# Second attention of a two-block transformer kernel: the halves of the output projection's weight chunks one head apart, the values ahead of the next transposes, the last queries copied at once

## The chip, the cores and the metric

One core of a Trainium2 chip runs the whole program. The metric is the device time in microseconds (us) of one execution. The time before the change is the median of three runs.

## What is computed

The reference runs 256 tokens of width 1024 through two blocks. The first has sliding-window and block attention and a feed-forward network. The second adds 16 meta tokens and has two layers of feed-forward networks around a pooling mixer in the first layer and a latent attention in the second. Only this latent attention is touched by the change:

```python
def mla_attention(h, w_dq, q_latent_norm, w_uq, w_o, k_nope, k_rope, v, cos, sin):
    cq = rmsnorm_2(h @ w_dq, q_latent_norm)
    q = (cq @ w_uq).reshape(B, L, N_HEADS, QK_NOPE + QK_ROPE)
    ...
        s = (jnp.einsum('bqhd,bkhd->bhqk', qn, k_nope)
             + jnp.einsum('bqhr,bkr->bhqk', qr, k_rope)).astype(jnp.float32) * sm_scale
        s = jnp.where(mask[None, None], s, jnp.finfo(jnp.float32).min)
        p = jax.nn.softmax(s, axis=-1).astype(v.dtype)
        return jnp.einsum('bhqk,bkhd->bqhd', p, v)
    ...
    return o @ w_o
```

There are 8 heads, 64 features without and 32 with rotary positions, 64 features of values, and the output projection w_o is 512 by 1024. After the attention comes the last feed-forward network ("ffn2_1"), and the final norm.

## The kernel before

**Weights.** All weights come from memory in chunks of 8 tiles of 128 by 128 (512 KB), in one order, into a ring of 8 raw buffers. SyncE issues the transfers in order and waits, before it reuses a buffer, until the low half of the chunk that lay in it has been made. A dense product is made of three passes: ScalarE copies a chunk to its high half (`split_hi`, line 1139), VectorE subtracts that from the raw chunk to get the low half (`split_lo`, line 1512), and TensorE multiplies high by high, high by the low half of the activations, and low by high (lines 615, 616 and 617). The halves lie in rings of 5 buffers. `split_hi(i)` waits for the transfer and for the last matmul that reads chunk i-5; `split_lo(i)` waits for `hi_done`; the matmuls wait for `lo_done`. In the attention, the places where the splits stand are written out by hand in each engine's order. The chunks are numbered here from the first of the output projection: chunks 0 to 3 are w_o, chunk -2 holds the rotary queries of heads 4 to 7 and part of the last keys, chunk -1 the rest of these keys and the last queries without rotary part, and chunks 4 and 5 are the first of ffn2_1.

**The order of the attention.** There is no planner; each engine runs its own list in order, and the loop `for i in range(MH + 2)` (MH = 8 heads) is written once for each engine, with semaphores between them.

- TensorE, step i: `scores2(i)` into a bank of PSUM (two banks, in turn), the transposes of head i-2 (`transposes2`, one bank, so it waits for `pT2_done` of the head before), and in even steps from 4 the values of a pair of heads (`values2`), which wait for the copied transposes of both heads and for the output of the pair before to be read out. Between them stand dense products that fill time: `uq_rope(1)` in step 0, `keys(1)` in step 1, `uq_nope(1)` (the queries of heads 4 to 7) in step 2, `out_proj(0)` in step 6, `out_proj(1)` in step 8. After the loop come half of `out_proj(2)`, `values2(3)`, the other half, and `out_proj(3)`.
- VectorE, step i: the maxima of head i's scores (line 2008) and the shift (line 2011), the reciprocals and the weights' scaling of head i-1 (lines 2017 and 2020), then whatever belongs to this step: `q_rope(1)` in step 0 (line 1973), `k_nope(1)` in step 2 (line 1968), `q_nope(1)` in step 3 (line 1964), the low half of a pair's output in odd steps from 5 (line 2029), and the low half of a chunk: 0, 1, 2, 3 in steps 0 to 3, 4 and 5 in steps 8 and 9. Chunk -1 is made just ahead of the loop.
- ScalarE, step i: the copy of the transposes of head i-2 (`pT2`, line 1467), the exponentials of head i (line 1474), then `k_nope(1)` in step 1, `q_nope(1)` in step 2 (line 1439), the high half of a pair's output in even steps from 4 (line 1484), and the high half of the same chunk as VectorE in the same step.
- `scores2(i)` waits for the exponentials of head i-2, and `scores2(4)` also for both halves of the `q_nope(1)` copies (ScalarE takes the even heads and VectorE the odd ones, after it). `transposes2(h)` waits for the scaled weights of head h. `exponentials` of head i wait for the shift, and from head 4 on for the transposes that free the buffer of the weights. From head 4 on the `pT2` copy also waits for the values of two pairs before.
- GpSimd adds the rotary parts of heads 4 to 7 (line 2183) after `q_rope(1)`.

Of the kernel before, what the change touches and what calls it, by code (L numbers as in the profile page):

```python
# [30 lines left out]
MH, ROPE = 8, 32  # L31
# [358 lines left out]
def build_program(nc, xT, metaT, vecs, consts, bands, bias_oh, bias_rows, wstream, scratch, outT):  # L390
# [6 lines left out]
    with ctx:  # L397
# [147 lines left out]
        weights2 = lambda h, n: p2[:, h // 2 % 2, p2_at(h, n):p2_at(h, n) + KW[n]]  # L545
        turned = lambda ap: ap.rearrange("p h (b t) -> p h b t", b=2)[:, :, ::-1, :]
        in_blocks = lambda ap: ap.rearrange("p h (b t) -> p h b t", b=2)
        WO_SPLITS = {i: i for i in range(4)}
        WO_SPLITS.update({MH: 4, MH + 1: 5})
        wo_out = lambda t: G[plan.pair["wo_a" if t < 4 else "wo_b"]][:, t // 2 % 2, t % 2 * SEQ:(t % 2 + 1) * SEQ]  # L550
        wo_left = lambda t: plan.left_dve["wo_a"] - 3 + t
        POOL_SPLITS = {0: 3, 1: 4, 4: 5, 6: 6}
# [38 lines left out]
        def tensor_program(e):  # L591
# [416 lines left out]
            def scores2(i):  # L1008
                bank = A[(i + 1) % 2]
                if i == 0:  # L1010
                    e.wait_ge(left_act, plan.left_act["uk0"])
                    e.wait_ge(left_dve, plan.left_dve["uk0"])
                    e.wait_ge(khead_rope, 1)
                    e.wait_ge(rows_set, 2)
                    e.wait_ge(q_var, 1)
                elif i == 1:
                    e.wait_ge(mix_var, 1)
                else:
                    e.wait_ge(exp2_done, i - 1)
                if i == 4:  # L1020
                    e.wait_ge(left_act, plan.left_act["uqn1"])
                    e.wait_ge(left_dve, plan.left_dve["uqn1"])
                if i < 2:
                    e.wait_ge(qrot_done, i + 1)
                else:
                    e.wait_ge(qrot_pool, i - 1)
                for n in (1, 0):
                    m = e.matmul(bank[:, OFF[n]:OFF[n] + KW[n]], qhead[:, i, n * P:(n + 1) * P], khead[:, i, KEYS(i, n)], start=True, stop=True)  # L1028
                m.then_inc(scored2, 1)
# [21 lines left out]
            def values2(p):  # L1051

                o = o2_of(p)
                if p == 0:
                    e.wait_ge(vm_act, 1)
                    e.wait_ge(vm_dve, 1)
                else:
                    e.wait_ge(o2_lo, p)
                e.wait_ge(pT2_done, 2 * p + 2)
                def meta(n):  # L1060
                    rows = slice(n * HD, n * HD + 2 * META)
                    return e.matmul(o[:, n * P:(n + 1) * P], v_meta[rows, p * P:(p + 1) * P], pT2[rows, (2 * p + 1) % 4, 3 * P:4 * P], start=n == 0, stop=n == 1, skip_group_check=True)
                meta(0).then_inc(meta_first, 1)
                for h in (2 * p, 2 * p + 1):
                    oh_, cols = o[h % 2 * HD:(h % 2 + 1) * HD, :], slice(h * HD, (h + 1) * HD)
                    e.matmul(oh_[:, 0:SEQ], v2[:, 0, cols], pT2[:, h % 4, 0:SEQ], start=False, stop=False, skip_group_check=True)
                    e.matmul(oh_[:, P:SEQ], v2[:, 1, cols], pT2[:, h % 4, SEQ:384], start=False, stop=False, skip_group_check=True)
                e.wait_ge(meta_first, p + 1)
                m = meta(1)
                m.then_inc(valued2, 1)  # L1070
# [20 lines left out]
            for i in range(MH + 2):  # L1091
                if i < MH:
                    scores2(i)
                if i >= 2:
                    transposes2(i - 2)
                if i >= 4 and i % 2 == 0:
                    values2((i - 4) // 2)
                if i == 0:
                    uq_rope(1)
                if i == 1:  # L1100
                    keys(1)
                if i == 2:
                    uq_nope(1)
                if i == 6:
                    out_proj(0)
                if i == MH:
                    out_proj(1)
# [20 lines left out]
        def scalar_program(e):  # L1128
# [316 lines left out]
                e.activation(in_blocks(khead[0:HD, 4 * i:4 * i + 4:2, 0:SEQ]), turned(src[:, :, META:T]), ACT.Copy).then_inc(left_act, 1)  # L1445
            split_hi(plan.last["uv"])
            q_nope(0)
            split_hi(plan.last["uqr1"])
            k_nope(0)
            e.wait_ge(q_var, 1)  # L1450
            e.activation(qsc[:, 2:4], qsc[:, 0:2], ACT.Sqrt, scale=float(QK)).then_inc(root_done, 1)
            preload(ACT.Exp)
            split_hi(plan.last["uqn1"])
            e.wait_ge(mm_done, ended["uv"])
            e.activation(v2[:, 0, :], G[plan.pair["uv"]][:, 0, :], ACT.Copy).then_inc(left_act, 1)
            e.wait_ge(mm_done, ended["uv_meta"])
            e.activation(values_of_pairs(v_meta, 0), values_of_pairs(A[3], 0), ACT.Identity, scale=con[:, cat["meta_of"]:cat["meta_of"] + 1]).then_inc(vm_act, 1)

            first_wo = steps["wo"][0].i
            for i in range(MH + 2):  # L1460
                if i >= 2:
                    h = i - 2
                    w = 512 if h % 2 else 384
                    e.wait_ge(transposed2, h + 1)
                    if h >= 4:
                        e.wait_ge(valued2, (h - 4) // 2 + 1)
                    e.activation(pT2[:, h % 4, 0:w], A[2][:, 0:w], ACT.Copy).then_inc(pT2_done, 1)
                if i < MH:
                    st = stat[:, i % 4, :]
                    e.wait_ge(shift2_done, i + 1)  # L1470
                    if i >= 4:
                        e.wait_ge(transposed2, 2 * ((i - 4) // 2) + 2)
                    for n in (1, 0):
                        a = e.activation(weights2(i, n), A[(i + 1) % 2][:, OFF[n]:OFF[n] + KW[n]], ACT.Exp,
                                         bias=st[:, n:n + 1], scale=qsc[:, n:n + 1], accum_out=st[:, 2 + n:3 + n])
                    a.then_inc(exp2_done, 1)
                if i == 1:
                    k_nope(1)
                if i == 2:
                    q_nope(1)  # L1480
                if i >= 4 and i % 2 == 0:
                    p = (i - 4) // 2
                    e.wait_ge(valued2, p + 1)
                    e.activation(o2h[:, p, :], o2_of(p), ACT.Copy).then_inc(o2_hi, 1)
                if i in WO_SPLITS:
                    split_hi(first_wo + WO_SPLITS[i])
            e.wait_ge(valued2, MH // 2)
            e.activation(o2h[:, 3, :], o2_of(3), ACT.Copy).then_inc(o2_hi, 1)
            preload(ACT.Sqrt)
# [13 lines left out]
        def vector_program(e):  # L1503
# [458 lines left out]
            def q_nope(i):  # L1962
                e.wait_ge(left_act, plan.left_act[f"uqn{i}"])
                e.tensor_copy(qhead[0:HD, 4 * i + 1:4 * i + 4:2, :], G[plan.pair[f"uqn{i}"]][HD:P, :, 0:SEQ]).then_inc(left_dve, 1)
# [24 lines left out]
            e.wait_ge(q_var, 1)  # L1989
            e.wait_ge(root_done, ROOT["latent_q"])  # L1990
            e.reciprocal(qsc[:, 0:2], qsc[:, 2:4]).then_inc(rstd_done, 1)
            e.wait_ge(mm_done, ended["uv"])
            e.tensor_copy(v2[:, 1, :], G[plan.pair["uv"]][:, 1, :]).then_inc(left_dve, 1)
            e.wait_ge(mm_done, ended["uv_meta"])
            e.wait_ge(vm_act, 1)
            e.tensor_scalar(values_of_pairs(v_meta, 1), values_of_pairs(A[3], 1), con[:, cat["meta_of"] + 1:cat["meta_of"] + 2], None, ALU.mult).then_inc(vm_dve, 1)
            split_lo(plan.last["uqn1"])

            first_wo = steps["wo"][0].i
            e.wait_ge(rstd_done, RSTD["latent_q"])  # L2000
            for i in range(MH + 2):
                if i < MH:
                    bank, st = A[(i + 1) % 2], stat[:, i % 4, :]
                    e.wait_ge(scored2, i + 1)
                    if i >= 4:
                        e.wait_ge(weighted2, i - 3)
                    for n in (1, 0):
                        a = e.tensor_reduce(st[:, 6 + n:7 + n], bank[:, OFF[n]:OFF[n] + KW[n]], AX_X, ALU.max, negate=True)
                    a.then_inc(max2_done, 1)
                    e.wait_ge(max2_done, i + 1)  # L2010
                    e.tensor_tensor(st[:, 0:2], st[:, 6:8], qsc[:, 0:2], ALU.mult).then_inc(shift2_done, 1)
                if i == 0:
                    q_rope(1)
                if 1 <= i <= MH:
                    st = stat[:, (i - 1) % 4, :]
                    e.wait_ge(exp2_done, i)
                    e.reciprocal(st[:, 4:6], st[:, 2:4]).then_inc(recip2_done, 1)
                    e.wait_ge(recip2_done, i)
                    for n in (1, 0):
                        a = e.tensor_scalar(weights2(i - 1, n), weights2(i - 1, n), st[:, 4 + n:5 + n], None, ALU.mult)  # L2020
                    a.then_inc(weighted2, 1)
                if i == 2:
                    k_nope(1)
                if i == 3:
                    q_nope(1)
                if i >= 5 and i % 2:
                    p = (i - 5) // 2
                    e.wait_ge(o2_hi, p + 1)
                    e.tensor_tensor(o2l[:, p, :], o2_of(p), f(o2h[:, p, :]), ALU.subtract).then_inc(o2_lo, 1)
                if i in WO_SPLITS:  # L2030
                    split_lo(first_wo + WO_SPLITS[i])
            e.wait_ge(o2_hi, 4)
            e.tensor_tensor(o2l[:, 3, :], o2_of(3), f(o2h[:, 3, :]), ALU.subtract).then_inc(o2_lo, 1)

# [218 lines left out]
```

## Time and profile before

| | us |
|---|---|
| median of 3 runs | 1285.72 (1284.29 to 1287.08) |
| the profiled execution, time | 1284.93 |
| the profiled execution, span | 1283.5 |
| TensorE busy | 1239.3 (97%) |
| VectorE busy | 879.7 (69%) |
| ScalarE busy | 633.7 (49%) |
| mean granted TensorE clock over the span | 0.989 of full |

The span is the time from the first to the last recorded instruction; the time lies 1.4 us above it. "Busy" counts an engine's own instructions, not its waits. The names "PE", "DVE", "ACT", "POOL" and "SP" stand for TensorE, VectorE, ScalarE, GpSimd and SyncE; "PEld" is TensorE's weight load, which overlaps its matmuls. The times in the rows are microseconds from the start of the span. A line of the timeline gives the start, the length, the engine, the line of the program, and in brackets the idle time before it and who ended that. The attention loop runs from about 1031 to 1085 us.

### The profile page before, as it was taken

Reading aid. Unit: us, or ns where it says so; the run is one execution under the profiler, and the core shown is the slowest. Engines: PE = TensorE matmul, PEld = TensorE weight load, DVE = VectorE, ACT = ScalarE, POOL = GpSimd, SP = SyncE. Lnnn points to the kernel's source line nnn. Section 1 sums busy time; section 2 is a strip of 40 time slices with the busy share of each in tenths; the row PEclk is TensorE's granted clock in tenths of the full one; section 3 lists DMA queues with packets and bytes.
Section 4 is the critical chain, followed back from the end, with each engine's and each line's share of the span. In section 5 each row is a group of like instructions: output and inputs, shape, how many; then the busy total and the mean of one; then the engine's idle time right before and its main releaser. Section 6 shows DMA issues by size and latency. Waiting matters only on the chain.

```text
span 1283.5 us, 23765 instructions
## 1 busy us (share of the span) xinstructions
PE 1239.3 (97%) x9924; PEld 1208.7 (94%) x9924; DVE 879.7 (69%) x1239; ACT 633.7 (49%) x986; POOL 178.6 (14%) x177
## 2 busy tenths in 40 slices
PE   4999999999999999999999999999999979999997
PEld 3988899999999999999999999999999968999997
DVE  7789979877566766655766665666667664766653
ACT  5545545766444444443544454445454455554531
POOL 2024424000231000012200002210001311000021
PEclk9999999999999999999999999999999978999999
DMA  8986565657555555654355555555564531656550
GB/s 326 322 310 215 198 223 204 241 214 280 181 183 175 165 169 177 198 173 127 118 195 167 182 178 181 181 164 183 196 201 158 185 98 34 197 184 196 183 163 33
DMA packets 67570, 239.16 MB, mean 186 GB/s; under 512 B 7366, under 2 KB 9592, under 8 KB 67464
## 3 DMA queue, kind: packets, MB, share of 16 engines
q1 hardware_dynamic: 66872, 235.46, 55.1%
q0 software_dynamic: 592, 2.19, 0.5%
q8 instruction: 78, 1.28, 0.4%
q14 instruction: 28, 0.23, 0.1%
HBM read 236.55 MB, written 1.07 MB: 185 GB/s over the span
## 4 chain that ended last, share of the span: by engine, by line
PE 86%; DVE 7%; ACT 2%; issue 1%; POOL 1%; DVEq 0%; ACTq 0%
PE G L615 26%; PE G L616 25%; PE G L617 25%; DVE sb_wlo L1512 2%; PE A L760 1%; PE A L735 1%; PE A L615 1%; ACT sb_whi L1139 1%; PE A L617 1%; PE A L616 1%; PE A L1028 0%; DVE sb_xl L2037 0%; DVE sb_hidf L1601 0%; PE G L1083 0%; PE A L746 0%
## 5 line engine op out<-in xcount | busy, mean ns | idle before, releaser
L1512 DVE TENSOR_TENSOR sb_wlo<-sb_raw,sb_whi 128x1024 fp32r<-128x1024 f32 (+1 forms) x398 | 486.4, 1256 | 90.3 <-ACT sb_whi L1139 90.0
L615 PE MATMUL G<-sb_xh,sb_whi 128*128 128x256 f32 (+2 forms) x1752 | 497.0, 284 | 5.1 <-DVE sb_wlo L1512 2.2
L616 PE MATMUL G<-sb_xl,sb_whi 128*128 128x256 f32 (+2 forms) x1752 | 496.7, 284 | 0.0
L1139 ACT ACTIVATE sb_whi<-sb_raw 128x1024 fp32r<-128x1024 f32 (+1 forms) x398 | 405.0, 1043 | 183.7 <-PE G L617 166.3
L617 PE MATMUL G<-sb_xh,sb_wlo 128*128 128x256 f32 (+2 forms) x1752 | 495.3, 283 | 0.0
L615 PEld LDWEIGHTS G<-sb_xh,sb_whi 128*128 128x128 f32 x1752 | 329.7, 188 | 8.3 <-issue 2.6
L617 PEld LDWEIGHTS G<-sb_xh,sb_wlo 128*128 128x128 f32 x1752 | 329.4, 188 | 0.0
L616 PEld LDWEIGHTS G<-sb_xl,sb_whi 128*128 128x128 f32 x1752 | 329.1, 188 | 0.0
L615 PE MATMUL G<-sb_hh,sb_whi 128*128 128x256 f32 (+1 forms) x1056 | 299.0, 283 | 0.6 <-DVE sb_hh L1732 0.6
L617 PE MATMUL G<-sb_hh,sb_wlo 128*128 128x256 f32 (+1 forms) x1056 | 298.0, 282 | 0.0
L616 PE MATMUL G<-sb_hl,sb_whi 128*128 128x256 f32 (+1 forms) x992 | 280.3, 283 | 0.0
L615 PEld LDWEIGHTS G<-sb_hh,sb_whi 128*128 128x128 f32 x1056 | 198.4, 188 | 1.0 <-issue 0.5
L617 PEld LDWEIGHTS G<-sb_hh,sb_wlo 128*128 128x128 f32 x1056 | 198.4, 188 | 0.0
L616 PEld LDWEIGHTS G<-sb_hl,sb_whi 128*128 128x128 f32 x992 | 186.5, 188 | 0.0
L1365 ACT ACTIVATE sb_gu<-sb_gu 128x272 f32<-128x272 f32 (+1 forms) x88 | 37.4, 425 | 191.5 <-DVE sb_gu L1840 191.3
L1840 DVE TENSOR_TENSOR sb_gu<-G,sb_rstd 128x544 f32<-128x544 f32 (+1 forms) x84 | 59.4, 707 | 59.8 <-PE G L617 59.8
L2079 POOL TENSOR_TENSOR sb_sumsq<-sb_X 128x256 f32<-128x256 f32 (+1 forms) x6 | 3.7, 622 | 651.6 <-DVE sb_X L1570 651.6
L1846 DVE TENSOR_TENSOR sb_hidf<-sb_gu 128x272 f32<-128x272 f32 (+1 forms) x88 | 38.3, 435 | 50.2 <-ACT sb_gu L1365 50.2
L1849 DVE TENSOR_TENSOR sb_hl<-sb_hidf,sb_hh 128x272 fp32r<-128x272 f32 (+1 forms) x88 | 38.2, 434 | 43.3 <-ACT sb_hh L1367 43.3
L1367 ACT ACTIVATE sb_hh<-sb_hidf 128x272 fp32r<-128x272 f32 (+1 forms) x88 | 37.4, 425 | 50.7 <-DVE sb_hidf L1846 50.7
L2084 POOL TENSOR_TENSOR sb_sq<-sb_X 128x256 f32<-128x256 f32 (+1 forms) x41 | 31.4, 766 | 203.7 <-DVE sb_X L1570 203.7
L2089 POOL TENSOR_TENSOR sb_sumsq<-sb_sumsq,sb_sq 128x256 f32<-128x256 f32 (+1 forms) x41 | 44.8, 1094 | 3.2
(328 smaller groups left out, 1289.1 us busy)
## 6 DMA issues: line engine op xcount, KB each, us to landing
sb_raw<-in_wstream SPq DMA_DIRECT2D x438, 512.0 KB, 4.4
sb_raw<-in_wstream SPq DMA_DIRECT2D x8, 320.0 KB, 6.9
sb_bias<-bias_scratch POOLq DMA_DIRECT2D x1, 2048.0 KB, 16.3
sb_X<-in_xT SPq DMA_DIRECT2D x2, 512.0 KB, 6.4
out_T<-sb_X SPq DMA_DIRECT2D x4, 256.0 KB, 2.7
sb_con<-in_consts SPq DMA_DIRECT2D x1, 601.0 KB, 8.7
sb_band<-in_bands SPq DMA_DIRECT2D x1, 314.0 KB, 5.0
sb_vec<-in_vecs SPq DMA_DIRECT2D x1, 82.5 KB, 2.0
```

Of the source, the lines that this page charges most:

```text
L615: e.matmul(out, w_h, xs, start=k0 + s.kt == 0, stop=False)
L616: e.matmul(out, w_h, xr, start=False, stop=False)
L617: m = e.matmul(out, w_l, xs, start=False, stop=k0 + s.kt == ktotal - 1)
L1139: e.activation(whi[:, i % NSPLIT, 0:w], raw[:, c % NRAW, 0:w], ACT.Copy).then_inc(hi_done, 1)
L1365: e.activation(gu[:, b, 0, 0:n], gu[:, b, 0, 0:n], ACT.Silu).then_inc(silu_done, 1)
L1367: e.activation(hh[:, j * n:(j + 1) * n], hidf[:, b, 0:n], ACT.Copy).then_inc(hid_hi, 1)
L1512: e.tensor_tensor(wlo[:, i % NSPLIT, 0:w], raw[:, c % NRAW, 0:w], f(whi[:, i % NSPLIT, 0:w]), ALU.subtract).then_inc(lo_done, 1)
L1840: e.tensor_tensor(gu[:, b, :, 0:n], G[plan.pair[name]][:, :, 0:n], rb, ALU.mult).then_inc(left_dve, 1)
L1846: e.tensor_tensor(hidf[:, b, 0:n], gu[:, b, 0, 0:n], gu[:, b, 1, 0:n], ALU.mult).then_inc(hid_mul, 1)
L1849: e.tensor_tensor(hl[:, sl], hidf[:, b, 0:n], f(hh[:, sl]), ALU.subtract).then_inc(hid_lo, 1)
L2084: e.tensor_tensor(s, src, src, ALU.mult).then_inc(sumsq_done, 1)
L2089: e.tensor_tensor(sumsq[:, cols], sumsq[:, cols], s, ALU.add).then_inc(sumsq_done, 1)
```

## The change

Four things are done, and the arithmetic stays the same.

1. The places of the splits. The high half of chunk -1 is made ahead of the first key copy, its low half ahead of the copy of the value rows; the high half of chunk 0 is made ahead of the loop, and its low half between the two value copies. In the loop a chunk's high half and its low half stand in different steps: high halves of chunks 1 to 5 in steps 0, 3, 5, 7, 8 of ScalarE, low halves in steps 1, 4, 6, 8, 9 of VectorE.
2. TensorE: `values2` stands ahead of `transposes2` in even steps from 4.
3. ScalarE: in these steps the exponentials and then the `pT2` copy, instead of the copy first.
4. VectorE: `q_nope(1)` at the start of step 3 instead of at its end.

```diff
-        WO_SPLITS = {i: i for i in range(4)}
-        WO_SPLITS.update({MH: 4, MH + 1: 5})
+        WO_HIGH, WO_LOW = {0: 1, 3: 2, 5: 3, MH - 1: 4, MH: 5}, {1: 1, 4: 2, 6: 3, MH: 4, MH + 1: 5}
...
                 if i < MH:
                     scores2(i)
+                if i >= 4 and i % 2 == 0:
+                    values2((i - 4) // 2)
                 if i >= 2:
                     transposes2(i - 2)
-                if i >= 4 and i % 2 == 0:
-                    values2((i - 4) // 2)
...
             q_nope(0)
-            split_hi(plan.last["uqr1"])
+            split_hi(plan.last["uqn1"])
             k_nope(0)
...
             preload(ACT.Exp)
-            split_hi(plan.last["uqn1"])
+            first_wo = steps["wo"][0].i
+            split_hi(first_wo)
...
+            def turned_weights(h):
+                w = 512 if h % 2 else 384
+                e.wait_ge(transposed2, h + 1)
+                if h >= 4:
+                    e.wait_ge(valued2, (h - 4) // 2 + 1)
+                e.activation(pT2[:, h % 4, 0:w], A[2][:, 0:w], ACT.Copy).then_inc(pT2_done, 1)
+
+            def exponentials(i):
+                st = stat[:, i % 4, :]
+                e.wait_ge(shift2_done, i + 1)
+                if i >= 4:
+                    e.wait_ge(transposed2, 2 * ((i - 4) // 2) + 2)
+                for n in (1, 0):
+                    a = e.activation(weights2(i, n), A[(i + 1) % 2][:, OFF[n]:OFF[n] + KW[n]], ACT.Exp,
+                                     bias=st[:, n:n + 1], scale=qsc[:, n:n + 1], accum_out=st[:, 2 + n:3 + n])
+                a.then_inc(exp2_done, 1)
             for i in range(MH + 2):
-                if i >= 2:
-                    h = i - 2
...
+                values_first = i >= 4 and i % 2 == 0
+                if i >= 2 and not values_first:
+                    turned_weights(i - 2)
                 if i < MH:
...
+                    exponentials(i)
+                if values_first:
+                    turned_weights(i - 2)
...
-                if i in WO_SPLITS:
-                    split_hi(first_wo + WO_SPLITS[i])
+                if i in WO_HIGH:
+                    split_hi(first_wo + WO_HIGH[i])
...
             e.reciprocal(qsc[:, 0:2], qsc[:, 2:4]).then_inc(rstd_done, 1)
+            split_lo(plan.last["uqn1"])
             e.wait_ge(mm_done, ended["uv"])
             e.tensor_copy(v2[:, 1, :], G[plan.pair["uv"]][:, 1, :]).then_inc(left_dve, 1)
+            first_wo = steps["wo"][0].i
+            split_lo(first_wo)
             e.wait_ge(mm_done, ended["uv_meta"])
...
-            split_lo(plan.last["uqn1"])
...
             for i in range(MH + 2):
+                if i == 3:
+                    q_nope(1)
...
-                if i == 3:
-                    q_nope(1)
...
-                if i in WO_SPLITS:
-                    split_lo(first_wo + WO_SPLITS[i])
+                if i in WO_LOW:
+                    split_lo(first_wo + WO_LOW[i])
```

## Rows read from the trace of the kernel before

**Rows 1.** The page: busy time, and the granted clock in 40 slices (tenths).

```profile
PE 1239.3 (97%) x9924; PEld 1208.7 (94%) x9924; DVE 879.7 (69%) x1239; ACT 633.7 (49%) x986; POOL 178.6 (14%) x177
...
PEclk9999999999999999999999999999999978999999
```

**Rows 2.** Busy time by stretch of the attention, all engines; PEclk is the granted clock.

```profile
1031.60:1037.40 5.80, 5.80 (x43) 5.38 (x41) 3.48 (x7) 2.54 (x6) 1.71 (x3) 1.00 0.35 101
1037.40:1041.00 3.60, 1.09 (x10) 1.05 (x10) 2.42 (x7) 2.12 (x7) 1.99 (x2) 1.00 0.46 130
1041.00:1044.40 3.40, 3.40 (x16) 3.28 (x16) 2.75 (x8) 1.71 (x5) 0.00 (x0) 0.50 0.24 55
1044.40:1047.80 3.40, 1.26 (x9) 0.72 (x8) 2.19 (x4) 2.20 (x5) 0.00 (x0) 1.00 0.29 116
1047.80:1063.50 15.70, 13.59 (x49) 9.15 (x49) 7.70 (x27) 7.08 (x21) 0.00 (x0) 0.50 0.24 68
1063.50:1068.30 4.80, 4.80 (x23) 4.80 (x23) 0.00 (x0) 0.38 (x1) 0.00 (x0) 0.50 0.00 0
1068.30:1071.70 3.40, 2.46 (x18) 1.76 (x16) 1.79 (x7) 1.44 (x5) 0.00 (x0) 1.00 0.00 0
1071.70:1084.70 13.00, 13.00 (x102) 11.23 (x102) 5.71 (x12) 6.86 (x15) 0.40 (x1) 1.00 0.27 82
```

**Rows 3.** Timeline of TensorE, 83 to 88 and 1036 to 1072 us: around its waits.

```profile
85.96 0.39 PE L615 MATMUL G<-sb_xh,sb_whi 128*128 128x256 f32 x1 [1.51 <-DVE sb_wlo L1512]
...
1036.58 0.87 PE L1028 MATMUL A<-sb_khead,sb_qhead 98*128 98x272 f32 x4
1039.95 0.55 PE L1040 MATMUL A<-sb_con,sb_p 128*128 128x128 f32 x3 [2.50 <-DVE sb_p L2020]
...
1049.91 1.73 PE L1028 MATMUL A<-sb_khead,sb_qhead 98*128 98x272 f32 x4 [4.25 <-DVE sb_qhead L1964]
...
1068.58 0.87 PE L1028 MATMUL A<-sb_khead,sb_qhead 98*128 98x272 f32 x4
1069.28 0.49 PE L1040 MATMUL A<-sb_con,sb_p 128*128 128x128 f32 x3
...
1071.16 0.52 PE L1040 MATMUL A<-sb_con,sb_p 128*128 128x128 f32 x3 [0.94 <-DVE sb_p L2020]
```

**Rows 4.** Timeline of TensorE at full clock, 1071 to 1078 us: starts of the pieces.

```profile
1071.61 0.48 PE L1062 MATMUL A<-sb_pT,sb_v_meta 32*128 32x128 f32 x2
...
1073.24 0.38 PE L1083 MATMUL G<-sb_o2h,sb_whi 128*128 128x256 f32 x1
...
1076.15 0.49 PE L1040 MATMUL A<-sb_con,sb_p 128*128 128x128 f32 x3
...
1077.02 0.39 PE L1083 MATMUL G<-sb_o2h,sb_whi 128*128 128x256 f32 x1
```

**Rows 5.** Timeline of VectorE ahead of the loop and in it.

```profile
1030.37 0.69 DVE L1993 COPY sb_v<-G 128x512 f32<-128x512 f32 x1 [1.48 <-PE G L635]
1032.35 0.48 DVE L1996 TENSOR_SCALAR sb_v_meta<-A,sb_con 128x256 f32<-128x256 f32 x1 [1.29 <-ACT sb_v_meta L1457]
...
1036.86 1.23 DVE L1512 TENSOR_TENSOR sb_wlo<-sb_raw,sb_whi 128x1024 fp32r<-128x1024 f32 x1 [1.54 <-ACT sb_whi L1139]
...
1038.96 0.94 DVE L2020 TENSOR_SCALAR sb_p<-sb_p,sb_stat 128x272 f32<-128x272 f32 x2
...
1047.41 0.66 DVE L2008 TENSOR_REDUCE sb_stat<-A 128x1 f32<-128x272 f32 x2
...
1048.96 0.69 DVE L1964 COPY sb_qhead<-G 64x512 f32<-64x512 f32 x1
```

**Rows 6.** Timeline of ScalarE in the loop.

```profile
1044.59 0.58 ACT L1439 ACTIVATE sb_qhead<-G 64x512 f32<-64x512 f32 x1
...
1048.29 0.58 ACT L1474 ACTIVATE sb_p<-A,sb_stat,sb_qsc 128x272 f32<-128x272 f32 x1 [1.70 <-DVE sb_stat L2011]
...
1049.31 1.05 ACT L1139 ACTIVATE sb_whi<-sb_raw 128x1024 fp32r<-128x1024 f32 x1
```

More of the change, by code:

```diff
@@ L1457, in scalar_program @@
             e.activation(values_of_pairs(v_meta, 0), values_of_pairs(A[3], 0), ACT.Identity, scale=con[:, cat["meta_of"]:cat["meta_of"] + 1]).then_inc(vm_act, 1)
-            first_wo = steps["wo"][0].i
-            for i in range(MH + 2):
-                if i >= 2:
-                    h = i - 2
[L1463 to L1467, printed above, removed]
-                if i < MH:
[L1469 to L1476, printed above, removed]
+            def turned_weights(h):
[13 more added lines that the diff above has]
+                a.then_inc(exp2_done, 1)
+            for i in range(MH + 2):
+                values_first = i >= 4 and i % 2 == 0
+                if i >= 2 and not values_first:
+                    turned_weights(i - 2)
+                if i < MH:
+                    exponentials(i)
+                if values_first:
+                    turned_weights(i - 2)
                 if i == 1:
@@ L1996, in vector_program @@
             e.tensor_scalar(values_of_pairs(v_meta, 1), values_of_pairs(A[3], 1), con[:, cat["meta_of"] + 1:cat["meta_of"] + 2], None, ALU.mult).then_inc(vm_dve, 1)
-            split_lo(plan.last["uqn1"])
-            first_wo = steps["wo"][0].i
             e.wait_ge(rstd_done, RSTD["latent_q"])
             for i in range(MH + 2):
+                if i == 3:
+                    q_nope(1)
                 if i < MH:
```

## The prediction, made before the changed kernel was run

> **What bounds the kernel now.** I read the page first: TensorE is busy 97% of the span, no other engine over 69%, and the granted clock is full but for two slices near the end [rows 1]. So time can only be won where TensorE stands still or runs at its low clock, and nearly all of that lies in the attention that the change touches. Second, busy time by stretch [rows 2]: of the 53.1 us from 1031.6 to 1084.7 TensorE is busy 45.4 (the eight rows add up to that), so it stands still for 7.7. Its clock is 0.50, the 1.2 GHz level, from 1041.0 to 1044.4 and from 1047.8 to 1068.3, which is 23.9 us, and 1.00 (2.4 GHz) in the other stretches. Third, TensorE's timeline [rows 3], for what ends the idle time: 2.50 us ahead of the first transposes, at 1039.95, until VectorE has scaled the weights of head 0; 4.25 us ahead of the scores of head 4, at 1049.91, until VectorE has copied the queries; 0.94 ahead of the last even transposes. The sum is 7.69. The first two stand right before the two falls of the clock; after the 0.94, and after the 1.51 us at 86 us, it stayed at full. Fourth, why VectorE is late [rows 5]: it waits 1.54 us for the high half of chunk 0 (1036.86), then makes the low half (1.23), and only then takes the maxima of head 1 and scales head 0 (1038.96, with 0.94, done at 1039.90). The high half, 1.05 us [rows 6], stands behind ScalarE's exponentials in the same step, so each of the steps 0 to 3 holds exponentials, high half and low half one after the other. The last query copy comes at 1048.96 after all of that [rows 5].
>
> **Prices of the pieces.** TensorE at full clock, from start to start: scores 0.70 ahead of transposes [rows 3], about 0.6 ahead of dense work (an estimate: dense matmuls start sooner behind them); even transposes 0.45, odd ones 0.87, values 1.63, 24 matmuls of the output projection 2.91 [rows 3, 4], so 0.12 each: about 2.2 for a product of 18 matmuls (`uq_rope`, `uq_nope`) and, with 272 columns, 1.6 for the 12 of `keys`. VectorE: from the maxima of a head (1047.41) to the query copy (1048.96) is 1.55 for maxima, shift, reciprocals and scaling, 0.88 of it until the exponentials start at 1048.29; copies of 512 columns 0.69, output low half about 0.45 (nearest row: 0.48) [rows 5, 6]. ScalarE: exponentials 1.02 from start to start, high half 1.05, query copy 0.58; copied transposes of like size 0.5 to 0.6, output high half about 0.4 (estimate, half of the columns) [rows 6].
>
> **Part by part, along TensorE's list.**
>
> *Ahead of the loop.* Low halves of chunks -1 and 0, 2.4 us, now stand around VectorE's value copies. These wait 1.48 and 1.29 us, together 2.77 [rows 5], and both high halves are there by then (that of chunk -1 fills ScalarE's wait for the first keys, that of chunk 0 takes its place). So they cost nothing, and VectorE is free for head 0 at 1032.8 (1032.35 and 0.48), 1.2 earlier. Without that cover they would cost what they cost now. Slots: chunk 0 needs chunk -5 to be read, chunk -1 chunk -6; both are finished long before.
>
> *The first gap (2.50).* VectorE's rotary product follows `uq_rope(1)`, done about 1034.5, to 1035.3; maxima of head 1 to 1036.1; head 0, whose exponentials ended near 1034.8, is scaled by 1036.8, or 1037.2 at the 0.94 of row 1038.96. TensorE ends the scores of head 2 at 1037.45 (1036.58 and 0.87). The gap is gone; `uq_nope(1)` runs from about 1037.6 to 1039.8, scores 3 and transposes 1 to 1041.5.
>
> *The second gap (4.25).* VectorE: low half of chunk 1 to 1038.0, maxima of head 2 to 1038.8, scaling of head 1, key copy to 1040.2. ScalarE: exponentials of head 2 until 1039.9, query copy 1040.0 to 1040.6. VectorE's query copy stands first in step 3: 1040.6 to 1041.3. Scores 4 start about 1041.6: 0.2 us of waiting instead of 4.25. The maxima of head 3 wait behind that copy for at most 0.7; who waits for them are the exponentials of head 3 and scores 5, which TensorE reaches only at 1044.2.
>
> *Values first, exponentials before the copied transposes.* Values 0 need the copies of heads 0 and 1 only (1042.0), so they fill the time in which head 2 is scaled. What is late next is the copy of transposes 2, ahead of transposes 3: ScalarE has the copy of head 1, exponentials 3 (1042.2 to 1043.2), the high half of chunk 2 (to 1044.2), exponentials 4 (to 1045.2) and then this copy, to 1045.7. TensorE is through with scores 5 at 1044.8 and waits 1.05. Behind transposes 3 and scores 6, values 1 wait 0.3 for the output of pair 0 to be read out.
>
> *Steps 6 to 9.* Transposes 4, `out_proj(0)` (2.9), scores 7 and transposes 5 run to 1054.0. Values 2 now stand ahead of transposes 6 and need pair 1's low half, which VectorE makes in step 7, after the maxima of head 7 and the scaling of head 6: 1053.4 plus 1.5 plus 0.45 is 1055.4. TensorE waits 1.5. Then values 2, transposes 6, `out_proj(1)`, transposes 7, half of `out_proj(2)`, values 3, the other half and `out_proj(3)` without a wait: 1.63 + 0.4 + 2.85 + 0.87 + 1.42 + 1.63 + 1.42 + 2.85 = 13.1 from 1055.5, which is 1068.7. The high halves of chunks 2 to 5 wait for slots freed by the values' rows, `keys(1)`, `uq_nope(1)` and `out_proj(0)`, all past by then; the low halves are ready before `out_proj(2)`, `out_proj(3)` and the feed-forward network ask for them.
>
> *SyncE's queue.* A transfer waits for the low half eight chunks before. Low halves -1 to 3 all come earlier by the clock than before, those of 4 and 5 some 10 us ahead of the next network, as now, so no transfer comes late. GpSimd's four rotary additions only need the rotary product, which stays where it was.
>
> **The sum, twice.** By the walk TensorE ends at 1068.7 instead of 1084.7: 16.0 saved. By the stretches: 23.6 us of busy time lie at full clock and 21.8 at half [rows 2]. 23 matmuls in 4.80 us against 24 in 2.91 make the low clock dearer by a factor of 1.72 [rows 2, 4], so 21.8 becomes 12.7, and 9.1 are won. The old idle time is 7.7; the new is 0.2 + 0.1 + 1.05 + 0.3 + 1.5 = 3.15, about 1 of which the ends of the running matmuls cover, so 2.2. Saved: 9.1 + 7.7 - 2.2 = 14.6. I take 15.3, the middle. Nothing behind the loop differs: the feed-forward network hangs on the last output tiles. The profiled execution took 1284.9, which gives 1269.6; the median shown lies 0.8 above it: **1270.4**.
>
> **Rivals.**
>
> *A, my forecast: both gaps go and the clock stays full.* For it: the stretch from 1068.30 to 1071.70 holds scores, two groups of transposes and a wait of 0.94, 2.46 us busy of 3.40, and kept 1.00; so did 86 us with 1.51. My worst stretch, 1044.4 to 1047.8, is busy about 2.1 to 2.3, against 1.09 and 1.26 before the falls. Own range 1268.5 to 1272.5: no new waits at all would give 2.2 less; a copy or two later in steps 5 to 7 would give 1 or 2 more.
>
> *B, the clock falls once inside the loop*, at the wait of 1.05 or at that of 1.5. Against it, the same rows; for it, nothing between 1.26 and 2.46 us busy has been seen here. Before, the level came back after dense products, after 3.4 us (`uq_nope`) and within the 4.8 of `out_proj(0)`. So the fall would last through values, transposes and one output product: 4.9 us of work become 8.4, and the scores behind add 1: plus 3.5 to 5, 1274 to 1275.5. The Trainium skill, page "TensorE: Matmul & The Clock Gate", section "A second HAM failure mode: psum-queue depth-cycling", says that many short idles between groups of matmuls can be enough for the clock to swing; that speaks for B, and only a trace of the new order can show it.
>
> *C, the first gap stays in part.* If scaling head 0 comes 1 us or more later than I have it (its margin is 0.3 to 0.6), the clock falls at 1041 as now, and no dense product follows before `out_proj(0)`: low from 1041 to about 1056, 15 us at a loss of 1 - 1/1.72 = 0.42 each is 6.3, and 0.7 of waiting: 1277.5.
>
> *D, slower than before.* The clock falls and does not come back before the loop ends, since less dense work lies together. To eat 15.3 us it would have to be low for 36 us, against 23.9 now: from 1041 through `out_proj(0)`, `(1)` and `(2)` and beyond. Both times that a dense product ran at the low level the clock came back [rows 2], and four such products follow. 1287.
>
> *E, no difference.* Only if the waits I remove come back whole elsewhere: 2.50 and 4.25 are each one engine's queue, and I find no second work of that size in front of them.
>
> **Chances.** A 0.75, B 0.13, C 0.07, D 0.03, E 0.02. A measurement of this kernel can tell 0.2%, 2.6 us, from no change. Faster: A, B and C, 0.95; same 0.02; slower 0.03. The range takes in A with the ends of its bounds and B: 1268.0 to 1275.8; C, D and E are left out.
>
> **What would show it.** TensorE's timeline: no wait over 0.5 us ahead of the first transposes or the scores of head 4; waits of about 1 us ahead of transposes 3 and of 1.5 ahead of values 2; granted clock 1.00 from 1031 to the end. The output projection's last matmul ends near 1069 instead of 1084.7. The prediction is wrong if the clock column shows 0.50 anywhere in the loop, if VectorE waits for high halves ahead of its first two scalings, or if the next network starts with a wait that was not there.

## The result and the profile after

The changed kernel takes 1271.15 us, the median of 4 runs (1269.39 to 1272.84), against 1285.07 before on the same occasions (also 4 runs); the ratio is 0.9889, 95% interval 0.9871 to 0.9907. That is 13.9 us faster, 0.75 above the forecast of 1270.4 and inside its range. The profiled execution took 1271.05, with a span of 1269.6 us against 1283.5.

Busy time by stretch of the changed kernel, to be read against [rows 2]; the first four stretches are the same, the later ones are cut where the clock changes:

```profile
1031.60:1037.40 5.80, 5.80 (x44) 5.43 (x43) 4.54 (x13) 3.84 (x12) 1.83 (x3) 1.00 0.57 189
1037.40:1041.00 3.60, 3.60 (x29) 3.33 (x29) 3.50 (x8) 2.18 (x7) 1.95 (x2) 1.00 0.19 60
1041.00:1044.40 3.40, 2.57 (x18) 1.66 (x17) 3.04 (x12) 2.35 (x7) 0.00 (x0) 1.00 0.23 90
1044.40:1047.80 3.40, 2.98 (x19) 2.12 (x18) 3.27 (x11) 2.59 (x8) 0.00 (x0) 1.00 0.18 16
1047.80:1058.00 10.20, 9.02 (x69) 7.19 (x68) 6.07 (x19) 6.45 (x18) 0.00 (x0) 1.00 0.30 100
1058.00:1061.40 3.40, 3.40 (x18) 3.40 (x18) 2.23 (x3) 1.71 (x3) 0.00 (x0) 0.50 0.42 141
1061.40:1070.80 9.40, 9.40 (x75) 8.20 (x74) 2.17 (x6) 4.00 (x9) 0.40 (x1) 1.00 0.22 62
```

From 1037.4 to 1041.0 TensorE is now busy all the time, where it was busy for 1.09 us. The granted clock stays at 1.00 to 1058.0, falls to 0.50 for 3.4 us, and is back. All of the attention ends at 1070.8. Every wait of TensorE in it, from the timeline of the changed kernel, against [rows 3]:

```profile
1037.29 0.55 PE L1039 MATMUL A<-sb_con,sb_p 128*128 128x128 f32 x3
...
1042.27 0.94 PE L1027 MATMUL A<-sb_khead,sb_qhead 98*128 98x272 f32 x4 [0.83 <-DVE sb_qhead L1970]
...
1046.44 0.55 PE L1039 MATMUL A<-sb_con,sb_p 128*128 128x128 f32 x3 [0.41 <-ACT sb_pT L1464]
...
1055.92 0.48 PE L1061 MATMUL A<-sb_pT,sb_v_meta 32*128 32x128 f32 x2 [1.18 <-DVE sb_o2l L2036]
...
1071.17 0.35 PE L614 MATMUL A<-sb_xh,sb_whi 128*128 128x256 f32 x1 [0.28 <-issue]
```

The first transposes come at 1037.29 with no wait (2.50 before), scores 4 wait 0.83 (4.25 before), and two waits are new: 0.41 for the copy of transposes 2, ahead of transposes 3, and 1.18 for the low half of pair 1's output, ahead of values 2. 2.1 us after that last wait the clock falls. The next network starts at 1071.17 with the same 0.28 as before. I use the length from the start of scores 0 to this first matmul as the measure of the attention: 53.48 before (1031.57 to 1085.05), 39.66 after (1031.51 to 1071.17), so 13.8 of the 13.9 us of the span lie in it.

The timeline of VectorE in the changed kernel, against [rows 5]:

```profile
1030.31 0.69 DVE L2000 COPY sb_v<-G 128x512 f32<-128x512 f32 x1 [0.35 <-PE G L634]
1030.91 1.22 DVE L1518 TENSOR_TENSOR sb_wlo<-sb_raw,sb_whi 128x1024 fp32r<-128x1024 f32 x1
1032.29 0.48 DVE L2005 TENSOR_SCALAR sb_v_meta<-A,sb_con 128x256 f32<-128x256 f32 x1 [0.16 <-ACT sb_v_meta L1457]
...
1036.18 1.06 DVE L2029 TENSOR_SCALAR sb_p<-sb_p,sb_stat 128x272 f32<-128x272 f32 x2
1037.16 1.74 DVE L1518 TENSOR_TENSOR sb_wlo<-sb_raw,sb_whi 128x1024 fp32r<-128x1024 f32 x1
...
1041.32 0.69 DVE L1970 COPY sb_qhead<-G 64x512 f32<-64x512 f32 x1 [0.23 <-ACT sb_qhead L1438]
```

The two low halves went into the waits ahead of the value copies, which shrank from 1.48 and 1.29 us to 0.35 and 0.16. Head 0 is scaled 2.8 us earlier than before, but in 1.06 us, and the low half of chunk 1 takes 1.74 instead of 1.23. Beside them runs GpSimd, from the timeline of the changed kernel:

```profile
1035.28 4.21 POOL L2190 TENSOR_TENSOR sb_qhead<-sb_gu 32x256 f32<-32x256 f32 x4 [8.47 <-DVE sb_gu L1979]
```

### The profile page after: what moved, and what is told of

Same layout as the page of the kernel before. It is cut to its first block, busy times and chain, and to the rows that moved or that the text cites. A ratio compares the mean times of both kernels' runs of the same rounds, so it can differ in the third digit from the quotient of the medians.

```text
span 1269.6 us, 23765 instructions
## 1 busy us (share of the span) xinstructions
PE 1230.2 (97%) x9924; PEld 1202.3 (95%) x9924; DVE 879.4 (69%) x1239; ACT 633.4 (50%) x986; POOL 178.9 (14%) x177
## 4 chain that ended last, share of the span: by engine, by line
PE 87%; DVE 7%; ACT 1%; issue 1%; POOL 1%; DVEq 0%; ACTq 0%
PE G L614 26%; PE G L615 26%; PE G L616 26%; DVE sb_wlo L1518 2%; PE A L759 1%; PE A L734 1%; PE A L614 1%; PE A L616 1%; PE A L615 1%; DVE sb_xl L2044 0%; DVE sb_hidf L1607 0%; ACT sb_whi L1138 0%; PE A L745 0%; DVE sb_xl L1583 0%; PE G L1082 0%
## 5 line engine op out<-in xcount | busy, mean ns | idle before, releaser
L1576 DVE SCALAR_TENSOR_TENSOR sb_X<-G,sb_X 128x272 f32<-128x272 f32 (+1 forms) x32 | 12.4, 427 | 48.0 <-PE G L616 48.0
```

## The experiments

Eleven kernels ran, in three groups. Each group has its own runs of the kernel before on the same chip (medians 1285.15, 1285.72 and 1284.80). "Attention" below is the measure just defined, from each profiled execution; "gain" is the difference of the medians.

| run | median | ratio to before, interval | gain | attention |
|---|---|---|---|---|
| e1 splits alone | 1276.85 | 0.9939 (0.9925 to 0.9953) | 8.3 | 43.58 |
| e2 query copy alone | 1280.51 | 0.9959 (0.9946 to 0.9971) | 4.6 | 48.01 |
| e3 values' order alone | 1282.52 | 0.9975 (0.9965 to 0.9985) | 2.6 | 50.46 |
| e4 before, filled | 1276.86 | 0.9935 (0.9922 to 0.9947) | 8.3 | 45.37 |
| e5 changed kernel again | 1271.34 | 0.9888 (0.9874 to 0.9903) | 14.4 | 38.11 |
| e6 changed kernel, filled | 1269.51 | 0.9874 (0.9860 to 0.9889) | 16.2 | 38.14 |
| e7 projection ahead of values 2 | 1270.93 | 0.9882 (0.9867 to 0.9897) | 14.8 | 37.87 |
| e8 additions later | 1269.03 | 0.9868 (0.9851 to 0.9884) | 16.7 | 37.45 |
| e9 splits and query copy | 1270.87 | 0.9888 (0.9872 to 0.9905) | 13.9 | 38.49 |
| e10 one addition early | 1270.55 | 0.9883 (0.9868 to 0.9897) | 14.3 | 37.44 |
| e11 e10 and e7 together | 1269.65 | 0.9878 (0.9863 to 0.9892) | 15.1 | 37.21 |

### e4: is it the clock or the waits?

```diff
+            def filler(n):
+                e.wait_ge(vm_act, 1)
+                e.wait_ge(vm_dve, 1)
+                for _ in range(n):
+                    e.matmul(A[3][:, SEQ:2 * SEQ], cqh[:, 0, 0:P], cqh[:, 0, :], start=True, stop=True, skip_group_check=True)
...
                 if i < MH:
+                    if i == 4:
+                        filler(34)
                     scores2(i)
+                if i == 2:
+                    filler(20)
```

> The kernel of before with extra matmuls whose result nobody reads, in the two waits: 20 (about 2.3 us) ahead of the first transposes and 34 (about 4.0 us) ahead of scores 4. No wait is taken away. My theory (9.1 of the gain is the low clock): the clock stays at 1.00 through the attention and the kernel is 8 to 9.5 us faster although it does more work. Rival (the work at half clock was hidden behind the other engines' queues, so only the waits count): 0 to 2 us faster.

Measured: 8.3 us faster, with 54 matmuls more. Two stretches of this kernel (TensorE busy and instructions, clock, transfers); the first is the whole attention up to the last output products:

```profile
1031.00:1071.00 40.00, 37.54 (x277) 1.00 0.27 82
1071.00:1077.00 6.00, 5.67 (x49) 1.00 0.27 87
```

The clock is 1.00 all through, and the attention is 8.1 us shorter (53.48 less 45.37). The rival, 2 us at most, is out. But this is the price of the second low stretch only. From TensorE's timeline in this kernel:

```profile
1049.38 0.94 PE L1028 MATMUL A<-sb_khead,sb_qhead 98*128 98x272 f32 x4 [0.33 <-DVE sb_qhead L1974]
```

Scores 4 start 18.35 us after scores 0 (1031.03), and in the kernel before it was 18.34 (1031.57 to 1049.91). VectorE's queue up to the query copy set that start, at either clock, so the low stretch from 1041.0 to 1044.4 cost nothing there: what full clock saved in it became waiting. All of the 8.1 us lie behind scores 4.

### e1, e2, e3: the parts alone

e1 is the kernel before with the first change to the places of the splits (`WO_HIGH`, `WO_LOW`, chunk -1 and chunk 0 ahead of the loop), nothing else. e2:

```diff
             for i in range(MH + 2):
+                if i == 3:
+                    q_nope(1)
...
-                if i == 3:
-                    q_nope(1)
```

e3 is the kernel before with `values2` ahead of `transposes2` and with `exponentials` ahead of `turned_weights` in even steps from 4.

> Only the places of the weight splits are changed (part 1); the order on TensorE, the order on ScalarE and the query copy are those of before. My theory (each gap is a queue on VectorE, and the clock follows the gaps): the 2.50 us ahead of the first transposes goes, the 4.25 ahead of scores 4 shrinks to about 2, since the query copy now stands behind the maxima of head 3 and the scaling of head 2 (1.55 less 0.2 for the wait). 8 to 13 us faster than before, depending on whether a wait of 2 us lets the clock fall (then 8). Rival (the gain is the sum of independent parts, each worth its own wait): 2.5 to 4.5 us faster.

> Only the last query copy of VectorE is moved to the start of step 3 (part 4). My theory: the 2.50 us wait and the fall of the clock at 1041 stay; VectorE copies the queries at about 1045.2, right after ScalarE's copy, so the 4.25 us wait shrinks to about 0.5 and the second low stretch of 20.5 us goes or becomes one short one: 3.8 us of waiting and up to 7 us of clock, 6 to 10 us faster. Rival (independent parts): 3.5 to 4 us faster.

> Only parts 2 and 3: values ahead of the next transposes on TensorE, exponentials ahead of the copied transposes on ScalarE in those steps. Both big waits stay and stand ahead of the place of this order, so the clock stays low as before: my theory says within 1.5 us of before. Rival (the order of the values carries a large part): 4 us or more faster.

e1 gained 8.3, as expected of it: the first wait is gone, the second is 2.18, and the clock falls there. The stretches of e1 around it (all engines, as in the first group above):

```profile
1031.00:1042.80 11.80, 9.65 (x73) 8.73 (x71) 10.09 (x27) 8.32 (x24) 3.79 (x4) 1.00 0.41 129
1042.80:1053.10 10.30, 10.26 (x36) 7.17 (x36) 4.71 (x15) 4.39 (x13) 0.00 (x0) 0.51 0.18 52
1053.10:1074.00 20.90, 19.94 (x153) 16.66 (x151) 9.83 (x27) 10.69 (x25) 0.42 (x2) 1.00 0.25 76
```

10.3 us at the low level, through scores, transposes and values alone; the clock came back at 1053.1, ahead of `out_proj(0)`, which starts at 1054.9. So dense products are not needed for the clock to come back, although both returns seen before had come with one.

e2 gained 4.6, less than the 6 to 10 that I expected. The wait ahead of scores 4 fell only to 2.56, not to 0.5: the low half of chunk 2 stands at the end of VectorE's step 2, ahead of the copy, and it waits 1.18 us for ScalarE's high half first. The timeline of VectorE in e2:

```profile
1047.35 1.22 DVE L1512 TENSOR_TENSOR sb_wlo<-sb_raw,sb_whi 128x1024 fp32r<-128x1024 f32 x1 [1.18 <-ACT sb_whi L1139]
1048.49 0.68 DVE L1964 COPY sb_qhead<-G 64x512 f32<-64x512 f32 x1
```

The move of the copy does its work only where the splits are moved too.

e3 gained 2.6, where I had expected 1.5 at most. Its two big waits are those of before (2.50 and 4.23), so the gain is not a wait removed. What differs is the clock: low for 3.4, 10.2 and 3.4 us, 17.1 in all, against 23.9, and the mean clock of its 8 runs is 0.990 to 0.994 against 0.987 to 0.991 in the 12 of before. The last 3.4 us follow a wait of 1.17 ahead of values 2, as in the changed kernel. The stretch behind scores 4 lasted 10.2 us in e2 too, and 10.3 in e1, both with the old order, so this order is not needed for a short one. Whether it made the clock come back sooner here, the runs do not say.

### e9: two parts without the third

This is the changed kernel with `transposes2` ahead of `values2` again and `values_first = False`.

> Parts 1 and 4 of the change, with the old order of values and transposes on TensorE and ScalarE (parts 2 and 3 undone). My theory: both big waits are gone with these two parts, and the order of the values only moves where TensorE waits later (0.41 and 1.18 us now; in the old order something like 0.94 ahead of transposes 6 and a wait of about 0.5 to 1 for values 0 or transposes 2). Within 1 us of the changed kernel, either way. Rival (the order of the values carries gain of its own, as its 2.6 us when done alone suggest): 2 to 3 us slower than the changed kernel.

The ratio to before is 0.9888, against 0.9889 and 0.9888 for the changed kernel: the same. With the clock at full in both profiled executions, the attention is 38.49 here and 38.11 in e5, so the order of the values is worth 0.4 us once the two waits are gone. The 2.6 that it brought alone cannot be added to the rest: it went with 6.8 us less of low clock (23.9 to 17.1), and the other parts remove that stretch anyway.

### e5 and e6: what the new waits cost

e6 is the changed kernel with matmuls in the wait ahead of values 2:

```diff
+            def filler(n):
+                e.wait_ge(exp2_done, MH - 1)
+                for _ in range(n):
+                    e.matmul(A[1][:, 0:SEQ], cqh[:, 0, 0:P], cqh[:, 0, :], start=True, stop=True, skip_group_check=True)
...
                     scores2(i)
+                if i == MH:
+                    filler(9)
```

> The changed kernel again, so that the next three stand beside it on one chip. All theories: 13 to 15 us faster than before; runs in which the clock falls once after the 1.18 us wait ahead of values 2 (mean granted clock 0.996 or 0.997) lie 1.5 to 2 us above those in which it does not (0.998 or more).

> The changed kernel with 9 extra matmuls (1.06 us) whose result nobody reads, in the wait of 1.18 us ahead of values 2. The wait stays. My theory (that wait lets the clock fall, for 3.4 us, in most executions): the clock stays at 1.00 and the median is 1 to 1.7 us below that of the changed kernel, with a smaller spread. Rival (the fall comes from what else lies around there, the transposes and small matmuls): the clock still falls, same time as the changed kernel.

e6 is 1.8 us below e5, and its attention is 38.14, 1.5 less than the 39.66 of the first profile. But e5 itself, with the wait of 1.18 unfilled, kept its clock in the attention too: 38.11. So this pair does not show that the filling kept the clock up, nor that it is why the median of e6 is lower. The fall of e5 is elsewhere. The stretches of e5, all engines:

```profile
80.00:86.50 6.50, 4.99 (x34) 4.42 (x34) 4.53 (x14) 3.52 (x9) 1.97 (x2) 0.98 0.86 342
86.50:90.00 3.50, 3.50 (x18) 3.50 (x19) 3.40 (x10) 2.12 (x6) 0.83 (x2) 0.55 0.00 0
...
1033.00:1072.00 39.00, 36.28 (x267) 30.60 (x265) 26.20 (x69) 23.82 (x62) 4.79 (x6) 1.00 0.32 102
```

It lies right behind a wait of 1.51 us in the first block, the wait that the prediction took as proof that the clock stays [rows 3]; and the same was seen in the profiled executions of e2, e7, e10 and e11, five of thirteen. (The wait there is 1.49 to 1.51 us, but 1.72 in e8, which kept its clock, and in e10, which did not.) Ahead of values 2, waits of 1.17 in e3 and 1.18 in the first profile were followed by a fall, waits of 1.18 in e5, e8 and e10 were not. So waits of 1.2 to 1.7 us let the clock fall in some executions and not in others, in two places of this program, and the mean clock of a run (0.995 or 0.996 in all four of e5) does not tell in which. My expectation for e5 read it as one place; that was wrong. One fall costs 1.55 us (39.66 less 38.11).

### e7: another order ahead of values 2

```diff
             for i in range(MH + 2):
+                if i == MH:
+                    out_proj(1)
                 if i < MH:
                     scores2(i)
...
-                if i == MH:
-                    out_proj(1)
...
+                if i == 7:
+                    p = (i - 5) // 2
+                    e.wait_ge(o2_hi, p + 1)
+                    e.tensor_tensor(o2l[:, p, :], o2_of(p), f(o2h[:, p, :]), ALU.subtract).then_inc(o2_lo, 1)
...
-                if i >= 5 and i % 2:
+                if i >= 5 and i % 2 and i != 7:
```

> The changed kernel, but in step 8 the second part of the output projection stands ahead of values 2, and VectorE makes the low half of pair 1's output at the start of step 7 instead of its end, so that this projection can start at once. My theory: the wait of 1.18 us and the fall of the clock both go, 2.2 to 2.8 us faster than the changed kernel. Rival (the wait moves to the next pair's output, ahead of the half projection): the gain is under 1 us.

The wait of 1.18 is gone, but the attention is only 0.24 shorter than in e5 (37.87), and the median 0.4 lower. The size is the rival's, the place is another. From TensorE's timeline in e7:

```profile
1060.80 0.55 PE L1039 MATMUL A<-sb_con,sb_p 128*128 128x128 f32 x3
1061.93 0.55 PE L1039 MATMUL A<-sb_con,sb_p 128*128 128x128 f32 x3 [0.58 <-ACT sb_pT L1464]
```

Transposes 6 and 7 now follow each other with nothing between them, and they share one bank, so the second waits for the copy of the first. The projection that stood between them had hidden that copy.

### e8, e10, e11: GpSimd beside VectorE

```diff
             for h in range(2, MH):
                 i, r = h // 4, h % 4 * ROPE
                 e.wait_ge(left_dve, plan.left_dve[f"uqr{i}"])
+                if h == 4:
+                    e.wait_ge(lo_done, steps["wo"][0].i + 2)
```

This is e8; e10 has `h == 5` instead, and e11 is e10 with the edit of e7.

> The changed kernel, but GpSimd's four rotary additions wait until VectorE has made the low half of chunk 1, so that they do not run beside VectorE's first scaling and that low half. My theory (VectorE is slowed by GpSimd there: 1.06 for 0.57 and 1.74 for 1.23): these two take 0.57 and 1.23, the maxima of head 2 come 1.0 us earlier, and the wait ahead of scores 4 shrinks from 0.83 to under 0.4, if the additions, now about 1 us later, do not become the wait: 0.4 to 0.8 us faster than the changed kernel. Rival (the two are slow for another reason, such as the transfer or ScalarE): they stay at 1.06 and 1.74, and the time is the same or up to 1 us longer.

> The changed kernel, but the last three of GpSimd's four rotary additions (heads 5 to 7) wait until VectorE has made the low half of chunk 1; the one that scores 4 need runs at once. My theory: VectorE's first scaling and that low half take 0.57 and 1.23 (a little more for the first, if the early addition still runs beside it), scores 4 no longer wait for GpSimd, and the wait ahead of them is under 0.3: 0.6 to 1 us faster than the changed kernel in the stretch from scores 0 to scores 4, median about 1270.5 or less. Rival (the slowness is not GpSimd's): same stretch as in the changed kernel, 10.76 us.

> The last one and the projection ahead of values 2 together. My theory: the two gains add, 0.6 to 1 and 0.2 to 0.5 us, and with no wait over 0.6 in the attention the clock stays at full there: the lowest median of all, 1268.3 to 1269.8, against 1271.2 of the changed kernel. Rival: the earlier scores 4 only lengthen a later wait (ahead of transposes 3 or 7), and the time is that of the better one of the two.

VectorE's timeline in e10:

```profile
1038.30 0.57 DVE L2029 TENSOR_SCALAR sb_p<-sb_p,sb_stat 128x272 f32<-128x272 f32 x2
1038.79 1.22 DVE L1518 TENSOR_TENSOR sb_wlo<-sb_raw,sb_whi 128x1024 fp32r<-128x1024 f32 x1
...
1040.99 1.11 DVE L2029 TENSOR_SCALAR sb_p<-sb_p,sb_stat 128x272 f32<-128x272 f32 x2
```

and GpSimd's:

```profile
1037.41 0.72 POOL L2192 TENSOR_TENSOR sb_qhead<-sb_gu 32x256 f32<-32x256 f32 x1 [8.48 <-DVE sb_gu L1979]
1040.14 2.56 POOL L2192 TENSOR_TENSOR sb_qhead<-sb_gu 32x256 f32<-32x256 f32 x3 [2.01 <-DVE sb_wlo L1518]
```

Without the additions beside them the scaling takes 0.57 and the low half 1.22, in e8 as in e10; the scaling of head 1, beside which the three late additions run, takes 1.11 instead, against 0.57 in the other kernels. So it is GpSimd's work that makes VectorE's slower. The first addition of e10, which runs beside VectorE's maxima of head 1, takes 0.72 and slows nothing. From scores 0 to scores 4 it is 10.10 us in e10 and 10.11 in e8, against 10.77 in e5: 0.66 won, and the wait ahead of scores 4 is 0.30 and 0.31. In e8 it was GpSimd that ended it, in e10 VectorE's query copy, so keeping one addition early changed who is last, not when.

VectorE does not always lose. Single additions from GpSimd's timeline, the first in the kernel before, the others in the changed kernel:

```profile
1037.14 1.52 POOL L2183 TENSOR_TENSOR sb_qhead<-sb_gu 32x256 f32<-32x256 f32 x1
...
1037.01 0.80 POOL L2190 TENSOR_TENSOR sb_qhead<-sb_gu 32x256 f32<-32x256 f32 x1
...
1037.96 1.54 POOL L2190 TENSOR_TENSOR sb_qhead<-sb_gu 32x256 f32<-32x256 f32 x1
```

Before, VectorE's low half of chunk 0 had begun at 1036.86 [rows 5], ahead of the addition: it kept its 1.23, and the addition took 1.52. In the changed kernel the low half began at 1037.16, when an addition was under way: that addition took 0.80, the low half 1.74, and the next addition, begun beside it, 1.54. In these rows the one that began first kept its time or nearly so, and the other was held up.

e11 has the shortest attention of all, 37.21, 0.9 less than the changed kernel at full clock, and the two gains add (0.67 and 0.24). Its median of 1269.65 lies in the range I gave, but it is not the lowest of all, and whether it beats the changed kernel as a program stays open: the intervals of e5, e8, e10 and e11 overlap, and the 1.5 us of a fall at 86 us, which some executions have and others not, are larger than what tells the attentions apart. e8's lower median goes with four runs at a mean clock of 0.998, and its attention is no shorter than that of e10.

## Why the prediction was right

**The bound.** That all was to be won from two waits and the low clock behind them was right. The sum had 9.1 for the clock. e4 shows 8.1 for the second low stretch; the first cost nothing as long as VectorE's queue set the start of scores 4, and became worth having only with the waits gone. From scores 0 to scores 4 it is 10.77 us in e5 against 18.34, which is 7.6 less, where the waits there shrank by 5.9.

**Ahead of the loop, and the first gap.** As the walk had it: the two low halves cost nothing, transposes 0 at 1037.29 against the forecast of no wait from 1037.45. The margin of 0.3 to 0.6 in C was nearly used up: VectorE was done with head 0 at 1037.24, since the scaling took 1.06.

**The second gap.** 0.83 instead of 0.2. The term that was too small is VectorE's work under GpSimd's additions. The prediction named the 0.94 of the scaling, but walked on from the shorter time (1036.8) and took 1.23 for the low half, from rows in which VectorE had begun first; it was 1.06 and 1.74, and the maxima of head 2 came at 1038.82 instead of 1038.0. e8 and e10 show the cause; moving the additions won 0.66 us.

**The new waits.** Ahead of transposes 3 it was 0.41, not 1.05, and ahead of values 1 nothing: scores 4 came 0.7 later than in the walk, so ScalarE's queue was less behind. Ahead of values 2 it was 1.18, not 1.5, from the queue that the walk named (the low half of pair 1 behind the maxima of head 7 and the scaling of head 6). The sum of all four is 2.42 against 3.15.

**The sum.** At full clock the attention is 38.11 in e5, 15.4 less than before; the forecast was 15.3. Its two ways of counting, 16.0 and 14.6, lie on either side, and neither is right in its parts. The walk had 0.7 too much of waiting, and its scores too short: from the start of scores 4 to the end of scores 5 it had 3.2 us (1041.6 to 1044.8), and the changed kernel took 3.76 (1042.27 to 1046.03, 0.41 ahead of 1046.44), with 0.87 from scores 4 to values 0 where at most 0.70 was allowed. That 15.3, the middle of two counts, came so near is in part luck.

**Which case it was.** The forecast was that of A, a clock at full. The profile after shows B's event in B's second place, behind the wait ahead of values 2, but at 1.55 us instead of 3.5 to 5: the level was low for 3.4 us, not until an output product was through. In e5 A came true in the attention. By the prediction's own signs this is a miss: it called itself wrong if the clock column showed 0.50 anywhere in the loop, and the wait ahead of scores 4 is over its 0.5. The profiled execution was forecast at 1269.6 and took 1271.05, 1.45 more, about the price of one fall (1.55). The gain was forecast at 15.3 and measured at 13.9. The median lies only 0.75 above the forecast because the base helped: 0.8 had been added for the median of before over its profiled execution, and before was 1285.07 this time, not 1285.72. A fall seems to be in most executions of this kernel, there or at 86 us: seven of the eight runs of the changed kernel have a mean clock of 0.997 or less, the four profiled executions that fell nowhere have 0.998 or 0.999. The evidence taken against B, that the clock had stayed after the 1.51 us at 86, was one execution's luck, which e5 shows. The 0.13 for B was low: of the five profiled executions with a wait of 1.17 or 1.18 ahead of values 2, two fell behind it. C, D and E did not occur.

**The order of the values** was priced within the walk only. e9 shows that parts 1 and 4 carry all but 0.4 us of the attention. The sentence "what is late next" of that part was right.

## What to carry to other kernels

When TensorE's clock is low behind a wait, count the slower work as part of that wait's price, and measure it by filling the wait with matmuls that nobody reads: here 6.75 us of waiting in two places cost another 8.1. Then look where these lie: a low stretch ahead of a start that another engine's queue sets costs nothing until that queue is shorter. Two in-order queues that take turns on one chunk in the same step (high half, then low half) make each wait for the other; one step between them removed both. Do not price the parts of such a change alone and add them: 2.6 us for the order of the values became 0.4.

## What the runs showed of the hardware that was not expected

- Waits of 1.2 to 1.7 us let the granted clock fall to 0.50 for about 3.4 us in some executions of the same kernel and not in others (1.18 ahead of values 2: fell in the first profile, not in e5; 1.50 and 1.51 at 86 us: the other way round). One fall costs 1.55 us.
- The low level ended under scores, transposes and values alone in e1 (after 10.3 us) and in e2 (10.2), where before it lasted 20.5 us through like work and the first output product. Why is open.
- GpSimd's additions of 32 by 256 in SBUF and VectorE's work in SBUF hold each other up: the scaling of the weights took 0.94 to 1.11 instead of 0.57 and the low half of a chunk 1.74 instead of 1.23, but where the low half had begun first it kept its 1.23 and the addition took 1.52 instead of 0.73. The maxima read from PSUM beside them were not slowed (0.65).
